# The second weights of a streamed expert loop issued on ScalarE's DMA queue instead of SyncE's

## What is computed

```python
def expert_block(args):
    xb, e = args                                  # 128 rows of tokens, one of 32 experts
    hb = xb @ w_e1[e] + b_e1[e]                   # w_e1[e]: 1024 x 2048
    return clamped_swiglu(hb) @ w_e2[e] + b_e2[e] # w_e2[e]: 1024 x 1024

y = zeros((T, D)).at[row_tok].add(y_rows * row_gate[:, None])   # each token has 4 experts
h = layer_norm(DEEPNORM_ALPHA * h + y, ln2_g, ln2_b)
```

## Time and profile before

| | |
|---|---|
| median of 3 runs | 1546.01 us (1545.33 to 1546.18) |
| the profiled execution's own time | 1544.39 us |
| its span, first to last instruction | 1542.6 us |
| granted TensorE clock, mean | 0.996 |
| TensorE matmul busy | 1410.8 us (91% of the span) |
| VectorE busy | 679.6 us (44%) |
| ScalarE busy | 154.0 us (10%) |
| SyncE's DMA queue, share of 16 engines | 73.4% of the span, 457.68 MB |
| ScalarE's DMA queue | 0.6%, 3.56 MB |
| GpSimd's software queue | 3.0%, 16.64 MB |

### The profile page before, as it was taken

How to read it: one execution, slowest core, us unless ns; L and a number is a source line. 1 busy time by engine, 2 the same in 40 slices (tenths; PEclk the granted TensorE clock), 3 DMA queues, 4 the chain that set the end, 5 groups by cost and what they waited for, 6 DMA issues and landing times.

```text
span 1542.6 us, 29979 instructions
## 1 busy us (share of the span) xinstructions
PE 1410.8 (91%) x12414; PEld 715.5 (46%) x12415; DVE 679.6 (44%) x1216; ACT 154.0 (10%) x287; POOL 328.1 (21%) x389
## 2 busy tenths in 40 slices
PE   7999999999999998999986788898789899999987
PEld 6887444458874644443332223333233334444442
DVE  5177344333334764354344334443444334434455
ACT  4112322111110120000000000000000000000001
POOL 1060000000000044233323322332233222323210
PEclk9999999999999999999999999999999999999999
DMA  6533100263317599999999999999999999999997
GB/s 220 188 123 102 28 0 1 53 200 96 95 49 307 202 367 416 420 423 422 422 423 423 420 424 424 422 421 423 424 422 422 425 422 424 423 422 420 423 394 273
DMA packets 98102, 478.52 MB, mean 310 GB/s; under 512 B 14820, under 2 KB 61316, under 8 KB 72968
## 3 DMA queue, kind: packets, MB, share of 16 engines
q1 hardware_dynamic: 84064, 457.68, 73.4%
q0 software_dynamic: 12080, 16.64, 3.0%
q10 hardware_dynamic: 1912, 3.56, 0.6%
HBM read 471.17 MB, written 23.08 MB: 320 GB/s over the span
## 4 chain that ended last, share of the span: by engine, by line
PE 70%; DMA 23%; DVE 3%; issue 2%; another core or an unknown queue 1%; ACT 1%; POOL 0%; SPq 0%; DVEq 0%; POOLq 0%; ACTq 0%
PE ps L1962 23%; DMA big<-in_w_e 22%; PE ps L2007 14%; PE ps L1655 12%; PE ps L1858 4%; PE ps L1822 4%; PE ps L1643 3%; PE ps L1739 2%; PE ps L1788 2%; PE ps L1799 2%; PE ps L1757 1%; PE ps L1806 1%; PE ps L1767 1%; DMA rest<-x_rows,P 1%
## 5 line engine op out<-in xcount | busy, mean ns | idle before, releaser
L1962 PE MATMUL ps<-big,rest 128*32 128x512 f32 x5024 | 557.9, 594 | 73.1 <-DMA big<-in_w_e 53.6
L1962 PEld LDWEIGHTS ps<-big,rest 128*32 128x32 f32 x5024 | 167.2, 110 | 448.7 <-issue 439.4
L2007 PE MATMUL ps<-big,rest 128*32 128x256 f32 x4992 | 292.0, 381 | 29.2 <-DMA big<-in_w_e 23.6
L2007 PEld LDWEIGHTS ps<-big,rest 128*32 128x32 f32 x4992 | 174.4, 110 | 154.5 <-issue 50.3
L1484 DVE MEMSET stat<- 128x1 f32 x30 | 1.8, 59 | 468.9 <-PE ps L1962 468.9
L770 POOL DMA_INDIRECT rest<-x_rows,idx x120 | 147.3, 1228 | 57.2 <-issue 31.7
L786 POOL DMA_INDIRECT expert_rows<-rest,slot x120 | 119.2, 994 | 53.9 <-issue 28.4
L1029 ACT ACTIVATE rest<-rest 128x1024 f32<-128x1024 f32 x32 | 33.9, 1060 | 898.5 <-DVE rest L1463 743.0
L778 POOL COPY idx<-P 128x4 uint32 (+1 forms) x30 | 5.5, 185 | 437.7 <-DVE rest L1485 428.6
L746 POOL IOTA P<- 128x128 f32 x1 | 0.2, 243 | 349.8 <-DVE rest L1311 349.8
L1500 DVE TENSOR_TENSOR rest<-ps,rest 128x1024 f32<-128x1024 f32 x32 | 39.2, 1225 | 66.8 <-PE ps L2007 65.8
(11 more groups left out here) (329 smaller groups left out, 1240.0 us busy)
## 6 DMA issues: line engine op xcount, KB each, us to landing
big<-in_w_e SPq DMA_DIRECT2D x187, 2048.0 KB, 24.3
rest<-in_w_in SPq DMA_DIRECT2D x14, 1024.0 KB, 5.5
big<-expert_rows SPq DMA_DIRECT2D x4, 2048.0 KB, 14.7
gate_area<-in_w_in SPq DMA_DIRECT2D x8, 512.0 KB, 4.8
rest<-in_w_in SPq DMA_DIRECT2D x8, 512.0 KB, 4.8
big<-in_w_out SPq DMA_DIRECT2D x1, 4096.0 KB, 12.8
gate_area<-in_w_e SPq DMA_DIRECT2D x2, 2048.0 KB
X<-in_x SPq DMA_DIRECT2D x4, 512.0 KB, 9.4
```

The lines of the kernel that those rows point to most:

```text
L1962: last = mm(ps[TB * g:TB * (g + 1), h0 + b, :], rows[:, k, b, :], quarter_of(k, g), start=(k == 2 * order[0]), stop=(k == 2 * order[-1] + 1))
L2007: last = mm(ps[TB * g:TB * (g + 1), 4 + b // 2, YW * (b % 2):YW * (b % 2 + 1)], acts[:, k, b, :], rows_of(k, g), start=(first and k == 0), ...
```

## The change

For experts 3 to 30 the two halves of the second weights are issued by ScalarE, behind the load of the second bias in the same turn, on ScalarE's own DMA queue. The waits, the sizes, the buffers and the semaphores are the same. The first weights stay on SyncE's queue. The second weights of the first three experts, and of the last one, are issued where they were.

```diff
@@ -659,7 +659,6 @@
             load_w1(3, 3)
             with sp.Fori(3, n_it - 1) as it:
                 load_w1(it + 1, sp.snap((it + 1) % E))
-                load_w2(it, sp.snap(it % E))
             for u in range(W2_UNITS):
                 sp.wait_ge(w1_used, n_it * PAIRS + (u + 1 - PAIRS))
                 sp.dma_start(last_W2[:, W2_ROWS * u:W2_ROWS * (u + 1), :],
@@ -1048,8 +1047,13 @@
             act.wait_ge(w2_used, 2 * W2_UNITS)
             act.dma_start(gain[:], A["ln2_g"].broadcast_to([P, D])).then_inc(norm_rows_landed, 16)
             act.dma_start(bias[:], A["ln2_b"].broadcast_to([P, D])).then_inc(norm_rows_landed, 16)
-            with act.Fori(3, n_it) as it:
+            with act.Fori(3, n_it - 1) as it:
                 turn(it)
+                for u in range(W2_UNITS):
+                    act.wait_ge(w2_used, W2_UNITS * it - W2_UNITS + u + 1)
+                    act.dma_start(W2[:, W2_ROWS * u:W2_ROWS * (u + 1), :],
+                                  A["w_e2"][0, act.snap(it % E)].rearrange("(p a) n -> p a n", p=P)[:, W2_ROWS * u:W2_ROWS * (u + 1), :]).then_inc(w2_landed[u], 16)
+            turn(n_it - 1)
             act.wait_ge(b1_landed, n_it * 16 + 16)
             act.wait_ge(y_ready, n_it + 1)
             for g in range(2, CG):
```

## The result

The changed kernel takes 1558.81 us (median of 4 runs, 1558.33 to 1559.03); the kernel before took 1546.10 us in 4 runs beside it (1545.33 to 1546.83). The ratio is 1.0083, 95% interval 1.0069 to 1.0097: 12.7 us slower. The forecast was 1553.3 us, 7.3 us slower, with a range of 1548 to 1561. The direction held and the time lies in the range. The kind of both losses was right. The idle time inside the loop was put far too low, and the lower TensorE clock in the last turn was not foreseen.

What follows compares the result with a forecast made beforehand. The prediction took the loop to be bound by DMA weight bytes. Nothing for the issues, 6.3 us in the tail and 1.0 us of idle time made 7.3 us, forecasting 1553.3 us, range 1548 to 1561.

Steps and rivals of the forecast that it cites:

- The bound: Expert loop: full DMA engines moving weight bytes at 422 GB/s set the time, so who issues them gains nothing.
- The overtaking: Two weight queues: second-weight halves u0, u1 land before the next expert's first-weight pairs p1 to p3, costing at loop end.
- the waits before the second product would shrink: TensorE in the loop: waits before line 2007 shrink, those before line 1962 grow by about as much.
- The term of 6.3 us in the tail: Loop end: last first-weight pair p3 lands late, delaying expert 30's output; 6.3 us, middle of 4.2 and 8.3.
- the upper bound: Tail with TensorE on time at 1472 us: p3 lands at 1495.1, line 1500 starts 8.3 us later.
- the 6.0 of the lower: Tail with TensorE 7 us late: p3 lands at 1479 + 2 x 6.0, line 1500 starts 4.2 us later.
- By itself this costs nothing: ScalarE's issues behind the second bias: u0 about 6 us later, u1 about 2 us, at no cost.
- My term for idle time: DMA engines inside the loop, where TensorE is slower: 1 us of idle time, bounds 0 and 4.
- 15 less 10.2 is still above zero: Four-block turn: queued reserve of about 15 us, less up to 10.2 us, stays positive, so idle time near the lower bound.
- A higher rate: Rival, whole loop: two weight queues drive the DMA engines harder, giving about 1544 us or less; chance 0.06.
- the even share of the engines: DMA engines: queues alternate packet for packet, so each weight queue gets half while both hold work.
- held up by gathered rows: Rival, loop: token gather and scatter wait behind two weight packets instead of one, giving about 1580 us; chance 0.08.

Runs made afterwards that it cites:

- e4: Kernel before, with only the second-weight halves of experts 29 and 30 moved to ScalarE's queue: ratio 1.0056, 8.5 us over before.
- e3: Changed kernel with the halves of experts 29 and 30 back on SyncE's queue: ratio 1.0030, 4.3 us over the kernel before.
- e1: Changed kernel with the halves issued ahead of the second bias load instead of behind it: ratio 1.0077, 11.6 us over the kernel before.
- e7: Changed kernel with experts 3 to 28's halves issued ahead of the second bias, 29 and 30's on SyncE: ratio 0.9999 to the kernel before.

## Why the prediction was right, and what was too small

- **The bound.** The loop is bound by bytes, and two queues move them no faster: right, 422 GB/s at 1.01 in both, while the queues are full. The Trainium skill, in "DMA: Bandwidth & Descriptors", section "Issuing engines are not separate DMA queues", says that a second issuing engine saves issue time alone, as all transfers run interleaved on the same 16 engines. The rate here agrees. What follows from it for the time, no change, is 12.7 us off, because the section doesn't say what interleaving does to the order of landing.
- **The overtaking.** Right in kind and in place. The halves were there while p3 was missing, and the waits got fewer and longer. That the waits before the second product would shrink was wrong: they grew from 23.6 to 43.2 us and those before the first fell from 53.6 to 34.8. u1, issued late, is often last itself.
- **The term of 6.3 us in the tail** (bounds 4.2 and 8.3). For a loop that is on time, as in e4, the working of the upper bound came out for p3's start (1495.1 against 1495.06) and for the 8.4 us of VectorE behind it, though u1 was issued at 1481.0 us and not at 1472.4. It left out that the clock falls during the wait ahead of p3, 2.8 us more for its product: e4's trace has 10.9. So it is in part luck that the 8.5 of e4's medians is so near to 8.3. In the change itself the halves moved 7.9 us of transfers ahead of p3, between the 10.2 of the upper case and the 6.0 of the lower. So the middle was a fair choice for the order of landing; the clock, 2.7 us in the change's trace, was missing from the term.
- **"By itself this costs nothing, as four pairs of first weights are still outstanding then"** is the step that failed. It was read from a two-block turn. Near the four-block turn the reserve is gone, and there u0 is issued 4.5 us late while the engines run dry. My term for idle time, 1 us within 0 to 4, went by the reserve alone, without that lateness. It also left out of its own sum a figure that it names: "15 less 10.2 is still above zero" doesn't subtract the 7 us by which TensorE starts the stretch late. With them the reserve is 2.2 us short. In the change TensorE starts the three-block product at the head of that stretch at 1292.48 us where it was 1284.82, 7.7 us late. e3 measures 4.3 us by the medians and 7.2 by its trace, above the bound of 4. e1 shows that issuing sooner takes the loss around that turn from 7.3 to 4.4 us of transfers; of the rest the 2.2 us missing in the sum may explain a part.
- **The rivals.** A higher rate didn't come, and the even share of the engines held (80 packets against 80). No stretch shows VectorE held up by gathered rows: it stood idle for TensorE alone ahead of turning them.
- The forecast was 6.3 + 1.0. By the medians of e4 and e3 it is 8.5 + 4.3 for 12.7. The idle time inside the loop is the term that was too small by most: more than four times by e3's medians, and more by its trace.

## What to carry to other kernels

In this loop, which is bound by DMA bytes, a second queue gave no bandwidth, but it changed the order of landing, and a part of its price was due where the loop ends. Look in such a case at what the last transfer still has behind it. Cost a delayed issue at the turn where the reserve of outstanding transfers is smallest, not at a typical one, and subtract from the reserve all that draws on it. Try repairs of two losses together: here either alone left a third or nine tenths of the loss, and with both no loss could be measured.

## What was not expected of the hardware

The granted clock fell to 0.50 during many of TensorE's longer waits, as in the 6.82 us ahead of 1088.66 us. It did not in all: behind a wait of 3.66 us that ended at 1478.43 us it stood at 1.00, and behind one of 2.27 us that ended at 841.07 us it was 0.72 over 6 us. The old order had no wait for weights above 2.0 us from 700 to 1500 us and kept a clock of 1.00. In the change the products of one pair behind five waits of 3.75 to 6.82 us took 5.8 to 6.4 us in place of 3.64. Over the loop the mean clock was 0.96, and in e7 this cost nothing measurable: while the bytes were the bound, it did no harm that TensorE was slower.
